# Unscaled x in the first layer, early turns and split weights at the ends of four layers of a one-core kernel

## The reference, cut to what matters

```
x = x + diff_attention(norm(x))      # a0: q, k, v, gate products; 8 heads; rms norm of q and k per head; sub-norm; out product
x = x + conformer_conv(norm(x))      # b
x = x + mla(norm(x))                 # c
x = x + diff_attention(norm(x))      # a1
x = x + attn_conv_mixer(norm(x))     # h
x = x + (silu(h @ w_gate) * (h @ w_up)) @ w_down     # ffn, hidden width 3584
x = x + (gelu(y) * lru(conv(x_branch))) @ w_out      # r: recurrent, one scan over the tokens per channel
x = x + moe_swiglu(norm(x))          # moe: 8 experts, top 2, hidden width 3584
```

## Time and profile before

| what | value |
|---|---|
| median of three runs | 2113.69 us (2112.16 to 2113.93) |
| profiled execution, its own time | 2114.06 us |
| its span | 2112.2 us |
| mean granted TensorE clock | 0.971 |
| TensorE busy | 94% |
| VectorE busy | 75% |
| ScalarE busy | 59% |
| mean HBM rate | 236 GB/s |

### The profile page before, as it was taken

How to read it: one execution, slowest core, us unless ns; L and a number is a source line. 1 busy time by engine, 2 the same in 40 slices (tenths; PEclk the granted TensorE clock), 3 DMA queues, 4 the chain that set the end, 5 groups by cost and what they waited for, 6 DMA issues and landing times.

```text
span 2112.2 us, 26539 instructions
## 1 busy us (share of the span) xinstructions
PE 1981.7 (94%) x9460; PEld 1650.7 (78%) x9460; DVE 1585.0 (75%) x1946; ACT 1236.0 (59%) x1446; POOL 142.3 (7%) x209
## 2 busy tenths in 40 slices
PE   7988989899978799998889999999999999999998
PEld 6767867677768578887878878888888888888886
DVE  6664975867646654454778898888989889898986
ACT  5461135745644344433757767777777777777775
POOL 3113401322001000000000000000000000000000
PEclk9999999999989599999999999999999999999999
DMA  8422233325224145554249989999898989989894
GB/s 318 150 80 80 100 130 135 120 100 177 94 90 162 38 159 185 194 182 160 74 164 353 376 300 380 345 367 377 329 376 332 373 344 360 376 333 372 332 374 176
DMA packets 70518, 499.99 MB, mean 237 GB/s; under 512 B 8736, under 2 KB 8736, under 8 KB 10528
## 3 DMA queue, kind: packets, MB, share of 16 engines
q1 hardware_dynamic: 70432, 498.87, 62.9%
HBM read 497.79 MB, written 1.05 MB: 236 GB/s over the span
## 4 chain that ended last, share of the span: by engine, by line
PE 82%; DVE 9%; ACT 4%; issue 3%; POOL 1%; DMA 0%; DVEq 0%; SPq 0%; ACTq 0%
PE psum L940 24%; PE psum L942 23%; PE psum L941 23%; PE psum L1937 4%; DVE low L907 3%; ACT high L904 2%; PE psum L3103 2%; PE psum L3164 1%; PE psum L1945 1%; POOL small L1168 1%; PE psum L1184 1%; ACT h L1671 1%; DVE x L1275 0%; PE psum L1567 0%; PE psum L1953 0%
## 5 line engine op out<-in xcount | busy, mean ns | idle before, releaser
L907 DVE TENSOR_TENSOR low<-raw,high 128x2048 fp32r<-128x2048 f32 (+1 forms) x460 | 1046.9, 2281 | 299.9 <-ACT high L904 298.7
L904 ACT ACTIVATE high<-raw 128x2048 fp32r<-128x2048 f32 (+1 forms) x460 | 877.4, 1912 | 416.3 <-PE psum L942 392.0
L940 PE MATMUL psum<-high,yT_high 128*128 128x512 f32 (+1 forms) x1672 | 666.4, 399 | 37.1 <-issue 13.6
L942 PE MATMUL psum<-high,yT_low 128*128 128x512 f32 (+1 forms) x1672 | 655.4, 392 | 0.0
L941 PE MATMUL psum<-low,yT_high 128*128 128x512 f32 (+1 forms) x1672 | 654.9, 392 | 0.0
L940 PEld LDWEIGHTS psum<-high,yT_high 128*128 128x128 f32 x1672 | 317.0, 190 | 109.0 <-issue 29.8
L942 PEld LDWEIGHTS psum<-high,yT_low 128*128 128x128 f32 x1672 | 316.8, 189 | 67.4
L941 PEld LDWEIGHTS psum<-low,yT_high 128*128 128x128 f32 x1672 | 317.7, 190 | 61.7
L940 PE MATMUL psum<-high,hT_high 128*128 128x512 f32 (+2 forms) x560 | 221.8, 396 | 12.2 <-DVE h L1848 6.1
L942 PE MATMUL psum<-high,hT_low 128*128 128x512 f32 (+2 forms) x560 | 218.0, 389 | 0.0
L941 PE MATMUL psum<-low,hT_high 128*128 128x512 f32 (+2 forms) x560 | 217.6, 389 | 0.0
(11 more groups left out here) (349 smaller groups left out, 1745.8 us busy)
## 6 DMA issues: line engine op xcount, KB each, us to landing
raw<-in_moe_weights SPq DMA_DIRECT2D x336, 1024.0 KB, 4.9
raw<-in_weights SPq DMA_DIRECT2D x132, 1024.0 KB, 5.0
raw<-in_weights SPq DMA_DIRECT2D x2, 896.0 KB, 4.6
raw<-in_weights SPq DMA_DIRECT2D x2, 768.0 KB, 8.1
x<-in_x SPq DMA_DIRECT2D x2, 512.0 KB, 4.0
raw<-in_weights SPq DMA_DIRECT2D x2, 512.0 KB, 3.6
out_x<-x SPq DMA_DIRECT2D x1, 1024.0 KB, 6.3
const<-in_constants SPq DMA_DIRECT2D x1, 512.0 KB, 8.7
```

Of the source, the lines that this page charges most:

```text
L904: eng.activation(high, raw, ACT.Copy).then_inc(k.high_ready, 1)
L907: eng.tensor_tensor(low, raw, high.bitcast(F32), ALU.subtract).then_inc(k.low_ready, 1)
L940: pe.matmul(out, lhs.high, rhs.high, start=start, stop=False)
L942: return pe.matmul(out, lhs.low, rhs.high, start=False, stop=stop)
```

## The change

Five places, in the order of the program:

1. **Start.** x itself is transposed, without the scaling; the products of a0 come out unscaled. GpSimd makes the two epsilons (`half_eps`) that a1 already used, and the evictions of v and gate take the token's factor as their scale (`token_scale`). The first two granules are both split in quarters, the second right after the last parts; the rotary tables come after that.
2. **Differential layers.** In the last step the pieces go (1,1,0), (0,1,1), (1,1,1). ScalarE and VectorE split the last output granule in step 20 ahead of the eviction of the last output turn. VectorE adds out 2, out 1, out 3.
3. **Feed-forward.** `down` becomes two entries of the order; the last turns go between the two halves of down 5; `hiddenT` has two buffers.
4. **Recurrent.** The mixing runs on pairs of chunks (128x512 operations), the first two pairs ahead of the last four scans; the output product goes by channel half first; the adds, turns and parts are written out in the new order.
5. The steps of the affected granules follow.

```diff
-    ITEMS + 5: [("out", 0, 1, 1), ("out", 1, 1, 0), ("out", 1, 1, 1)],
+    ITEMS + 5: [("out", 1, 1, 0), ("out", 0, 1, 1), ("out", 1, 1, 1)],
@@ ffn_order
-            order += [("down", j - 1, None)]
-    return order
+            order += [("down", j - 1, 0), ("down", j - 1, 1)]
+
+    early = [("turn", FF_STEPS - 1, t) for t in range(TILES)]
+    order = [one for one in order if one not in early]
+    at = order.index(("down", FF_STEPS - 2, 1))
+    return order[:at] + early + order[at:]
@@
-UNSCALED = (2, 3, 5)
+UNSCALED = (0, 2, 3, 5)
@@ plan_granules, "ffn" and "r"
-                            before = ("up", j + 1, 1) if j < FF_STEPS - 1 else ("turn", j, 1)
+                        before = ("up", j + 1, 1) if j + half < FF_STEPS - 1 else ("turn", FF_STEPS - 1, 1)
-            out(layer, w["rg_w_out_2"][0])
+            a, step = w["rg_w_out_2"][0], banks.order[(layer, "out", 3)]
+            for half in range(2):
+                for n in range(2):
+                    last = (layer, "out", 2 * n + 1) if half == 1 else halves + 1
+                    halves += half == 0
+                    granules.append(Granule(rows(a, 4 * half, 4 * half + 4, 512 * n, 512), (4, 512), last, step + n * half))
@@ norm_scalar, behind the squares
+    if n == 0:
+        act.wait_ge(k.const_landed, 16)
+        high_parts(k, act, n, (0, 1))
+        split_first_piece(k, act, 0)
+        high_parts(k, act, n, (2, 3))
+        split_first_piece(k, act, 1)
+        ahead(k, act, ("norm", n, 3))
+        return
@@ norm_vector, behind the squares
+    if n == 0:
+        v.wait_ge(k.const_landed, 16)
+        low_parts(k, v, n, (0, 1))
+        split_first_piece(k, v, 0)
+        low_parts(k, v, n, (2, 3))
+        split_first_piece(k, v, 1)
...
+        rope_tables(k, v, None, b.q_tables, k.wide("a_q_norm_g", 0, A_QK))
+        rope_tables(k, v, None, b.k_tables, k.wide("a_k_norm_g", 0, A_QK))
+        ahead(k, v, ("norm", n, 3))
+        return
@@ norm_pool
-        if n in (2, 3):
+        if n in (0, 2, 3):
             steps.link(pool.tensor_scalar(k.half_eps[:, 0:2], k.ms, EPS, None, ALU.mult))
             steps.link(pool.tensor_scalar(k.half_eps[:, 2:4], k.ms, Q_EPS, None, ALU.mult))
@@ norm_tensor
+        for t in range(TILES):
+            pe.wait_ge(k.x_landed[t], 16)
+    else:
+        pe.wait_ge(k.h_ready, 2 * (n + 1 - sum(m < n for m in UNSCALED)))
+    rows = k.x if n == 0 else k.h
@@ products
-        if g + half > 0:
+        if g + half > 1:
             wait_split(k, pe, g + half)
...
-                if g + half == 0 and t == 0:
+                if g + half < 2 and t == 0:
@@ a_evict
-    scale = token_scale(k, act, 3, t) if layer == "a1" else 1.0
+    scale = token_scale(k, act, 3 if layer == "a1" else 0, t)
@@ a_attention_scalar, a_attention_vector: ahead of the last output's eviction
+        if s == ITEMS + 4:
+            ahead(k, act, k.banks.ticks[(layer, s)])
...
+        if s == ITEMS + 4:
+            ahead(k, v, k.banks.ticks[(layer, s)])
...
+    add_to_x(k, v, (layer, "out", 2), 0, 1)
     add_to_x(k, v, (layer, "out", 1), 1, 0)
     ahead(k, v, (layer, "out", 3))
     ahead(k, v, k.banks.ticks[(layer, "out", 0, 1)])
-    add_to_x(k, v, (layer, "out", 2), 0, 1)
     add_to_x(k, v, (layer, "out", 3), 1, 1)
@@ ffn_buffers (the two slots are the two halves of yT)
-    b.hiddenT = hidden_parts(k)
+    b.hiddenT = [hidden_parts(k, slot) for slot in range(2)]
@@ r_tensor
-    out_tensor(k, pe, "r", k.r_mixed)
+    for at, (half, n) in enumerate(((0, 0), (0, 1), (1, 0), (1, 1))):
+        wait_split(k, pe, g + at)
+        pe.wait_ge(k.r_mixed, 2 * (half + 1))
+        w = granule_parts(k, g + at, 4)
+        for t in range(TILES):
...
+            for c in range(4):
+                row = 4 * half + c
+                last = three_passes(pe, k.bank(name), k.yT[:, row, P * t:P * (t + 1)], w[:, c, :], row == 0, row == KC - 1)
...
+            if (half, n, t) == (1, 1, 0):
+                turn_x(k, pe, RAW_NORM["r"], (0, 1))
@@ r_scalar
+    for pairs in ((0, 1), (2, 3)):
+        for pair in pairs:
...
+            if pair >= 2:
+                ahead(k, act, ("r", "y", 3) if pair == 2 else ("r", "out", 0))
+        for pair in pairs:
+            two = slice(2 * pair, 2 * pair + 2)
+            act.wait_ge(k.r_gated, pair + 1)
+            act.activation(k.yT.high[:, two, :], b.padded[:, two, 0:SEQ], ACT.Copy).then_inc(k.r_high_ready, 1)
+    ahead(k, act, ("r", "out", 3))
+    ahead(k, act, ("norm", RAW_NORM["r"], 0))
+    half_squares(k, act, "r", 0)
+    high_parts(k, act, RAW_NORM["r"], (0, 1))
@@ r_vector
+    def mixed(pairs):
+        v.wait_ge(steps.sem, steps.done)
+        for pair in pairs:
+            gated(pair)
+        for pair in pairs:
+            low(pair)
...
     ahead(k, v, ("r", "y", 2))
+    mixed((0, 1))
+    ahead(k, v, ("r", "y", 3))
     scans(range(4, R_HEADS))
...
+    ahead(k, v, ("r", "out", 0))
+    mixed((2, 3))
+    ahead(k, v, ("norm", RAW_NORM["r"], 0))
+    for i in range(3):
+        add_to_x(k, v, ("r", "out", i), i % 2, i // 2)
+    low_parts(k, v, RAW_NORM["r"], (0, 1))
+    add_to_x(k, v, ("r", "out", 3), 1, 1)
```

More of the change, by code:

```diff
@@ L452, in plan_banks @@
         banks.plan(("r", kind, i), Banks.LONG if kind == "y" else Banks.SHORT)
-    out("r")
+    for i in range(4):
+        banks.plan(("r", "out", i), Banks.LONG)
+    for part in range(2):
+        banks.plan(("norm", RAW_NORM["r"], part), parts=True)
     norm(7)
@@ L568, in plan_granules @@
                 if kind == "down":
-                    for half in range(2):
-                        row = FF_STEP * j + 2 * P * half
-                        src = packed(w["ffn_w_down_2"][0][row:row + 2 * P, :])
-                        if j == FF_STEPS - 1 and half == 1:
-                            granules.append(Granule(src, (2, D), (layer, "out", 3), banks.order[(layer, "out", 3)]))
-                        else:
-                            halves += 1
-                            before = ("up", j + 1, 1) if j < FF_STEPS - 1 else ("turn", j, 1)
-                            granules.append(Granule(src, (2, D), halves, banks.order[(layer,) + before]))
+                    half = t
+                    row = FF_STEP * j + 2 * P * half
+                    src = packed(w["ffn_w_down_2"][0][row:row + 2 * P, :])
+                    if j == FF_STEPS - 1 and half == 1:
+                        granules.append(Granule(src, (2, D), (layer, "out", 3), banks.order[(layer, "out", 3)]))
+                    else:
+                        halves += 1
+                        before = ("up", j + 1, 1) if j + half < FF_STEPS - 1 else ("turn", FF_STEPS - 1, 1)
+                        granules.append(Granule(src, (2, D), halves, banks.order[(layer,) + before]))
         if layer == "r":
@@ L1183, in norm_tensor @@
                 first = SEQ * (c % 2) + P * t
-                last = pe.transpose(k.bank(("norm", n, i))[:, first:first + P], k.h[:, t, P * c:P * (c + 1)], k.ident)
+                last = pe.transpose(k.bank(("norm", n, i))[:, first:first + P], rows[:, t, P * c:P * (c + 1)], k.ident)
         k.fill(last, ("norm", n, i))
@@ L2759, in r_tensor @@
             k.fill(last, name)
-    out_tensor(k, pe, "r", k.r_mixed)
+    for at, (half, n) in enumerate(((0, 0), (0, 1), (1, 0), (1, 1))):
+        wait_split(k, pe, g + at)
+        pe.wait_ge(k.r_mixed, 2 * (half + 1))
+        w = granule_parts(k, g + at, 4)
+        for t in range(TILES):
+            name = ("r", "out", 2 * n + t)
+            if half == 0:
+                k.take(pe, name)
+            for c in range(4):
+                row = 4 * half + c
+                last = three_passes(pe, k.bank(name), k.yT[:, row, P * t:P * (t + 1)], w[:, c, :], row == 0, row == KC - 1)
+            if half == 1:
+                k.fill(last, name)
+            elif t == 1:
+                last.then_inc(k.half_done, 1)
+            if (half, n, t) == (1, 1, 0):
+                turn_x(k, pe, RAW_NORM["r"], (0, 1))
 def r_scalar(k, act):
@@ L2882, in r_vector @@
     ahead(k, v, ("r", "y", 2))
+    mixed((0, 1))
+    ahead(k, v, ("r", "y", 3))
     scans(range(4, R_HEADS))
-    v.wait_ge(steps.sem, steps.done)
-    for c in range(KC + 1):
-        if c < KC:
-            gated(c)
-        if c >= 1:
-            low(c - 1)
-    out_vector(k, v, "r")
+    ahead(k, v, ("r", "out", 0))
[5 more added lines that the diff above has]
+    add_to_x(k, v, ("r", "out", 3), 1, 1)
 SLOTS = P
```

122 lines of the change are left out of this document (56 added, 66 removed).

## The result

| | before | after |
|---|---|---|
| median of the runs | 2113.81 us (4 runs, 2112.16 to 2116.40) | 2095.37 us (4 runs, 2094.06 to 2097.96) |
| ratio after / before, 95% interval | | 0.9913 [0.9901, 0.9924] |
| profiled execution, its span | 2114.06 us, 2112.2 us | 2095.38 us, 2093.5 us |
| mean granted TensorE clock | 0.971 | 0.974 |

The changed kernel is faster by 0.87%. The forecast was 2091.4 us with a range of 2086.5 to 2099: the time lies inside, 4.0 us above the forecast.

What follows compares the result with a forecast made beforehand. TensorE, busy for 94% of the span, was taken as the bound, with gains only at joints between layers: 3.6 + 5.6 + 1.9 + 7.0 + 4.5 = 22.6 us off 2114.06 gave 2091.4 us, range 2086.5 to 2099.

Steps and rivals of the forecast that it cites:

- rival (c): Start, second differential layer's end, recurrent end: VectorE's queue takes more, 4.5 us less gained, 2095.9 us; chance 0.05.
- Here a queue takes half of it back: Second differential layer's end: VectorE's splits for the next layer stand ahead of the last adds, leaving 1.9 us gained.
- rival (d): Expert layer starts earlier but waits for its first loads until the old time, 2112 to 2114 us; chance 0.03.
- (e): Rival: slower, the clock stays low through an attention, up to 63 us more, 2154 us at worst; chance 0.04.
- the one that credits the clock: Low-clock stretches behind removed waits go too: 1.65 us first differential layer, 2.3 feed-forward end, 1.7 recurrent end.
- rival (a): Low-clock stretches at three layer ends only move elsewhere, 5.6 us stay lost, 2097.0 us; chance 0.14.
- wrong if low-clock stretches are as many as before: Sign for the whole kernel: the forecast is wrong if the number of low-clock stretches does not fall.
- a0: First differential layer's end: waits of 1.56 and 3.07 us and a low-clock loss of 1.65 shrink, 5.6 us gained.
- Feed-forward: Feed-forward end: the 4.7 us wait and 2.3 us of low clock go, 7.0 us gained.
- Recurrent: Recurrent end: 6.0 us of waiting and low clock go, 1.5 of new idle time comes, 4.5 us gained.
- Start: Kernel start: transposes no longer wait for scaling, second granule comes without a stop, 3.6 us gained, ends 1.5 and 4.
- rival (b): Start: the first products run at the low clock, which costs 1.7 us, 2093.1 us; chance 0.04.

Runs made afterwards that it cites:

- h_queue: Changed kernel with only one granule of the next layer split ahead of the second differential layer's last add: 2091.52 us, ratio 0.9899 to the kernel before.
- ffn_only: Only the feed-forward edits on the kernel before: 2108.46 us, ratio 0.9974.
- r_only: Only the recurrent layer's edits on the kernel before: 2110.73 us, ratio 0.9982.
- start_only: Only the edits of the start on the kernel before: 2111.58 us, ratio 0.9986.
- after_again: The changed kernel run again with no edit: 2094.24 us, ratio 0.9916 to the kernel before.
- r_scans: Changed kernel with two of the last four scans ahead of VectorE's split of the second output granule: 2091.49 us, ratio 0.9895 to the kernel before.
- all_three: Changed kernel with the edits of h_queue, r_scans and warm together: 2085.31 us, ratio 0.9870 to the kernel before.
- warm: Changed kernel with 12 TensorE matmuls on a constant before the constants land: 2093.37 us, ratio 0.9904 to the kernel before.

## Why the prediction was right, and where it was not

The forecast's case came about, 4.2 us smaller than it was priced (18.4 instead of 22.6). The number alone decides nothing: it lies nearest to rival (c)'s 2095.9, whose mechanism did not occur.

**What was right.** First transpose near 7.5 (6.86), no wait into the second granule. One wait at each differential layer's end, 0.85 us by the forecast's times and measured 1.26 and 1.27, so its sign "no wait over 1 us" failed: the split began 3.01 us after its buffer's last piece began, not 2.75, and from its start to the matmul it was 0.14 us more. "Here a queue takes half of it back", 1.9 us for a1: against the first profile TensorE's end came 4.0 us earlier, the queue took 2.0, and 2.0 were left; `h_queue` gave 3.0 more by shortening that queue. (The forecast's 602.5 for the pieces of a1 would be 602.3 by its working for a0.) No yT_low wait at the feed-forward end (7.0 against 7.1, and the low halves ended 0.7 us before they were wanted, forecast 1). "1.55 us of new idle time" in the recurrent output: 1.32. The expert layer at 129.94 of 130, so rival (d) fell. Rivals (c) and (e) did too: VectorE had the second granule in time, and the attentions of the differential layers had no new low stretch of length.

**The step that failed** is the one that credits the clock. The terms hold 1.65 us of it for a0, 2.3 for the feed-forward end and 1.7 for the recurrent end, 5.6 in all, read from one execution as if the low stretches belonged to the waits ahead of them. Without this credit the sum is 17.0 us, 2097.1, which is rival (a), 2097.0. Measured was 2095.4: of the 5.6 us only 1.4 came back, as a net of gains and losses by place, and rival (a) was nearer to the truth than its chance of 0.14 says. The forecast's own sign says so too: "wrong if low-clock stretches are as many as before". They are: the first profile has 16 low stretches (124 us), the unchanged kernel's second 20 (114 us), the changed kernel 17 (111 us).

- *a0:* the stretch at 171.0 wasn't in the second execution of the unchanged kernel; its a0 was 1.5 us shorter with no edit. Against that one the change gains 4.9 - 1.5 = 3.4 in a0, just the 3.37 us of waits. In a1 it gains 2.0 + 1.4 = 3.4, which is not the waits come through: TensorE's end is 5.3 us earlier there, since that execution had its low stretch in front of it, and the queue keeps 2.0. So that a1 measured what was forecast holds against the first execution only, and the extra 1.4 hides part of what the other terms lack.
- *Feed-forward:* the second execution had one low stretch there (990.0 to 993.4), not two, and was 0.6 shorter. The credit of 2.3 is 1.7 in it. `ffn_only` gained 5.9 us in the runs, between the ends 4.7 and 7.3.
- *Recurrent:* both executions had the stretch and the change removed it, but the profiles of the changed kernel and of `r_only` lose 1.6 and 1.2 us in the expert layer that follows. In the changed kernel the clock is low from 1083.3 to 1090.1 and again at 1226.6 above.
- *Start:* 3.6 lies between two cases that both occur: 2.9 with the first products at the lower level (rival (b), which was given 0.04) and 4.5 to 4.8 at the upper (`start_only`, `after_again`, `h_queue`, `r_scans`; 4.1 in `all_three`, whose first transpose was at 7.40). Removing the waits was worth more than the sum had, because the constants were there at 6.86, not 7.49 (of such differences the unchanged kernel has some too: its second execution had the first product at 14.04, not 14.50).

The rule that rival (b) rested on (the Trainium skill, "TensorE: Matmul & The Clock Gate", Part 4: PE-mode transpose: transposes don't count as the activity that releases the clock) doesn't decide this. `start_only` had nothing but float32 transposes ahead of the product at 11.38, and that product and the next had the full pace; the changed kernel had the same, and was slow until 14.95. The Trainium skill, "TensorE: Matmul & The Clock Gate", Part 1: The HAM clock gate, says that there are two levels and a warm-up that differs from run to run. The traces here agree: of the twelve profiles without matmuls ahead, nine have the first products at the full pace and three have them slow.

**What stays open.** Why the low stretches fall where they do in an execution. That the credit is partly lost is measured (the parts alone, and the unchanged kernel's second execution); where each microsecond went can't be settled from single profiles, since two executions of one program differ by as much as the difference looked for. The times of the runs don't separate it either, since the runs of one kernel spread over 2 to 7 us. Their clocks say a little more. The span times one less the mean granted clock is the most that the low level can have cost in a run. It is 56.6 us in the mean of the 52 runs of the kernel before beside the experiments (clock 0.9732), and 54.4 us in the mean of the nine of the changed kernel (0.9740), so at most some 2 us came back, not 5.6. The profiled execution that the forecast was read from had 0.971, as low as the lowest of those 52.

The forecast's range ends at 2099, while its own low ends add up to 2100.0; nothing hung on it.

## What to carry to other kernels

Price a removed wait by the wait, and credit nothing for the clock behind it until a second execution of the same program has shown the low stretch in the same place; profile the unchanged kernel twice before explaining differences of a few microseconds by layer, and compare the granted clocks of all runs. When a wait stands behind an engine's queue, look first at the order in that queue: one condition on one granule took 3.1 of 4.7 us of waiting away, the early split alone was not measurably worse than the reordering with it, and two splits moved behind an add gave 3 us that the change had left. The parts at separate joints added up here (18.6 against 18.4, as far as runs with some 2 us either way can tell).

## What the runs showed of the hardware that was not expected

- The same wait has a low stretch behind it in one execution and none in another: a wait of 2.30 us before 1244.41 with 0.50 from 1246.0, one of 2.31 us before 1244.48 with 1.00; 3.07 us at the end of a0 with 0.51 behind it, and 3.07 us with 1.00. In such a stretch TensorE did 10 matmuls (at 1226.6 and 1246.0), where it did 19 and 17 at the upper level. Not all of that reached the end: the expert layers of five profiles with the most low stretches (10.2 us of matmuls in them instead of 3.4) were 1.2 to 2.0 us longer than the first profile's, those of five others with 6.8 us by 0 to 1.3.
- Two executions of one program differed by -1.4 to +1.7 us in layer after layer, and by 0.1 in the span (2112.2 and 2112.3).
- Matmuls that TensorE did ahead (`warm`) made the transposes nearly twice as fast (1.97 us instead of 3.67). The products after a gap of 2.32 us were slow again all the same; in `all_three`, after 2.16 us, they were not.
- The attention of the mixer layer h runs at the lower level for most of 48 us in the unchanged and in the changed kernel. Nothing here touches it, and it is the largest loss to the clock in the profile. The stretch view of the kernel before, and of the changed one 9.3 us earlier:

```profile
689.80:737.60 47.80, 36.90 (x120) 26.71 (x121) 32.33 (x134) 16.81 (x68) 0.00 (x0) 0.50 0.06 23
```

```profile
680.50:728.30 47.80, 33.39 (x117) 24.47 (x118) 33.58 (x137) 16.81 (x68) 0.00 (x0) 0.57 0.08 27
```

The difference between the two (0.50 and 0.57) goes with the 1.7 us that h gains in the ledger: `ffn_only`, low in the whole of this stretch as the first profile was, gains nothing in h, and the second execution of the unchanged kernel, with part of it at the upper level, gains 1.7 as well.
